# Attention weights scaled by ScalarE, head by head, at the head of the next slot, instead of by VectorE

## The reference

```python
s = jnp.einsum('btkgd,bjkd->bkgtj', qb, kc) * scale            # compressed keys
p_cmp = jax.nn.softmax(jnp.where(valid, s, NEG_INF), axis=-1) * valid
o_cmp = jnp.einsum('bkgtj,bjkd->btkgd', p_cmp, vc)
...
p = jax.nn.softmax(jnp.where(smask, s, NEG_INF), axis=-1)      # selected blocks
o_slc = jnp.einsum('bkgtn,bktnd->btkgd', p, vs)
...
p = jax.nn.softmax(jnp.where(wmask, s, NEG_INF), axis=-1)      # window
o_win = jnp.einsum('bkgtn,bnkd->btkgd', p, vw)
o = gb[..., 0:1] * o_cmp + gb[..., 1:2] * o_slc + gb[..., 2:3] * o_win
```

## Time and profile before

| | |
|---|---|
| median of 3 runs | 2523.26 us (2515.41 to 2525.65) |
| the profiled execution | 2526.35 us |
| its span, first to last instruction | 2524.6 us |
| busy in the span: PE, DVE, ACT, POOL | 2376.2 (94%), 1912.4 (76%), 1300.5 (52%), 277.4 us (11%) |
| mean granted clock of TensorE | 0.975 |
| slots 27 to 40 (layer 0) | about 303 to 443 us |
| slots 27 to 40 (layer 1) | about 1528 to 1661 us |

### The profile page before, as it was taken

One profiled execution on the slowest core, in us unless ns is written; L12 is line 12 of the kernel. 1 busy time (PEld: TensorE's weight loads), 2 busy tenths in 40 slices (PEclk: granted clock), 3 DMA queues, 4 the chain that ended last, 5 costly groups with the idle time before them and its releaser, 6 DMA issues.

```text
span 2524.6 us, 39922 instructions
## 1 busy us (share of the span) xinstructions
PE 2376.2 (94%) x13810; PEld 2060.3 (82%) x13810; DVE 1912.4 (76%) x2756; ACT 1300.5 (52%) x2117; POOL 277.4 (11%) x425
## 2 busy tenths in 40 slices
PE   4898889979999999999979999999899999999998
PEld 3788878757888888888869998886688888888886
DVE  7989987889999999766678976568897665565555
ACT  5265556446455455444466556654644444444444
POOL 1133211111111111000002130001010000000000
PEclk9998999999999999999989999999999999999999
DMA  9997858786998899777754764359596555556554
GB/s 389 398 334 276 301 200 266 257 318 236 345 352 321 324 340 331 272 266 269 273 212 143 262 237 161 115 201 355 205 354 219 186 187 183 186 188 187 194 193 151
DMA packets 197049, 643.04 MB, mean 255 GB/s; under 512 B 27249, under 2 KB 49905, under 8 KB 190913
## 3 DMA queue, kind: packets, MB, share of 16 engines
q1 hardware_dynamic: 125058, 421.72, 46.7%
q0 software_dynamic: 51264, 205.04, 22.9%
q10 hardware_dynamic: 20608, 14.72, 1.9%
HBM read 626.68 MB, written 14.71 MB: 254 GB/s over the span
## 4 chain that ended last, share of the span: by engine, by line
PE 75%; DVE 11%; DMA 6%; ACT 5%; issue 2%; SPq 1%; ACTq 0%; DVEq 0%; POOLq 0%
PE ps L1246 25%; PE ps L752 18%; PE ps L1247 13%; PE ps L735 10%; DMA ring<-stream 4%; DVE w_lo L1836 3%; PE ps L1126 3%; DVE ada_w L1842 2%; DVE mix L1836 2%; PE ps L800 2%; ACT w_hi L1307 1%; DMA ada_w<-ada_d 1%; SPq L535 1%; PE ps L1229 1%; PE ps L954 1%
## 5 line engine op out<-in xcount | busy, mean ns | idle before, releaser
L1836 DVE TENSOR_TENSOR w_lo<-ring,w_hi 128x1024 fp32r<-128x1024 f32 x720 | 893.8, 1245 | 485.9 <-ACT w_hi L1307 482.7
L1307 ACT ACTIVATE w_hi<-ring 128x1024 fp32r<-128x1024 f32 x720 | 761.4, 1059 | 837.4 <-PE ps L1247 351.1
L1246 PE MATMUL ps<-hT,w_hi 128*128 128x512 f32 x2688 | 947.3, 398 | 0.0
L1247 PE MATMUL ps<-hT,w_lo 128*128 128x256 f32 x2688 | 754.3, 281 | 0.0
L1246 PEld LDWEIGHTS ps<-hT,w_hi 128*128 128x128 f32 x2688 | 504.8, 188 | 124.7 <-DVE w_lo L1836 0.7
L1247 PEld LDWEIGHTS ps<-hT,w_lo 128*128 128x128 f32 x2688 | 507.9, 189 | 0.0
L735 PE MATMUL ps<-hT,w_hi 128*128 128x256 f32 x2176 | 414.7, 292 | 17.4 <-DVE w_lo L1836 15.8
L1842 DVE SCALAR_TENSOR_TENSOR ada_w<-ada_w,cs_row 128x1024 f32<-128x1024 f32 (+1 forms) x332 | 409.7, 1268 | 8.5 <-DMA ada_w<-ada_d 8.5
L735 PEld LDWEIGHTS ps<-hT,w_hi 128*128 128x128 f32 x2176 | 349.6, 197 | 28.1 <-issue 25.1
L735 PE MATMUL ps<-hT,w_lo 128*128 128x256 f32 x1088 | 312.9, 288 | 0.0
L605 POOL DMA_DIRECT2D ada_w<-ada_d x256 | 135.2, 528 | 1074.5 <-DVE ada_w L1842 1067.9
(11 more groups left out here) (306 smaller groups left out, 2420.2 us busy)
## 6 DMA issues: line engine op xcount, KB each, us to landing
ring<-stream SPq DMA_DIRECT2D x746, 512.0 KB, 4.5
ada_w<-ada_d POOLq DMA_DIRECT2D x320, 512.0 KB, 6.2
ada_w<-ada_d POOLq DMA_DIRECT2D x12, 1024.0 KB, 9.3
ada_lo<-ada_d POOLq DMA_DIRECT2D x10, 1024.0 KB, 11.9
ada_hi<-ada_d POOLq DMA_DIRECT2D x10, 1024.0 KB, 10.8
mix<-stream SPq DMA_DIRECT2D x14, 512.0 KB, 15.6
xs<-x SPq DMA_DIRECT2D x2, 2048.0 KB, 11.0
s_in_w<-mix ACTq DMA_DIRECT2D x8, 512.0 KB, 3.7
```

Source lines behind the costliest of these rows:

```text
L1246: pe.matmul(ps[:, bank, :], w_hi[:, s, ks], hT[:, k, :, :], start=k == 0, stop=False)
L1247: m = pe.matmul(ps[:, bank, SEQ:2 * SEQ], w_lo[:, s, ks], hT_hi[:, k, :], start=False, stop=k == KT - 1)
L1307: s.activation(w_hi[:, c % SPLIT, :], ring[:, at % RING, :], ACT.Copy).then_inc(hi_ready, 1)
L1836: return v.tensor_tensor(o, a, b, op)
```

## The change

For items of kind 1 and 2 the last product of `weighted` is taken from DVE. DVE now signals a new semaphore, `ns_w`, after the product of reciprocal and gate. ACT, in the next slot (28+m), behind its first `w_head` and ahead of `in_tile`, waits for `ns_w` and multiplies the exponentials head by head: four Copy instructions in place, with the column of `att_s` as the per-row scale. The last raises `ns_p`, for which the transposes wait as before. Items of kind 0 stay on DVE as they were. Since eight DVE instructions per layer no longer raise DVE's own step counter, its count falls from 210 to 202.

```diff
+        ns_w = Signal("ns_w", NI - NI // 3)
...
+                def weights_scaled(n):
+
+                    g, qt, kind = ITEMS[n]
+                    if kind == 0:
+                        return
+                    nk = (qt + 1) * P
+                    ns_w.wait(s, l, n - n // 3)
+                    for h in range(GQ):
+                        m = s.activation(pr[:, n % 2, h, 0:nk], pr[:, n % 2, h, 0:nk], ACT.Copy, scale=att_s[:, n % 2, 8 + h:9 + h])
+                    ns_p.by(m)
+
...
                     w_head(2 * n + AHEAD)
+                    if 0 <= n - ITEM_TILE - 1 < NI:
+                        weights_scaled(n - ITEM_TILE - 1)
                     in_tile(n)
                     w_head(2 * n + AHEAD + 1)
...
                     step(v.reciprocal(st3[:, 8:12], st3[:, 4:8]))
-                    step(tt(st3[:, 8:12], st3[:, 8:12],
-                            gates_t[:, qt, :].rearrange("p (h c) -> p h c", c=3)[:, GQ * g:GQ * (g + 1), kind], ALU.mult))
-                    w3 = st3[:, 8:12].unsqueeze(2).to_broadcast([P, GQ, nk])
+                    (ns_w.by if kind else step)(
+                        tt(st3[:, 8:12], st3[:, 8:12],
+                           gates_t[:, qt, :].rearrange("p (h c) -> p h c", c=3)[:, GQ * g:GQ * (g + 1), kind], ALU.mult))
                     if kind == 0:
+                        w3 = st3[:, 8:12].unsqueeze(2).to_broadcast([P, GQ, nk])
                         step(tt(p3, p3, w3, ALU.mult))
                         ok = K("cmp_valid", qt * NC, (qt + 1) * NC).unsqueeze(1).to_broadcast([P, GQ, nk])
                         ns_p.by(tt(p3, p3, ok, ALU.mult))
-                    else:
-                        ns_p.by(tt(p3, p3, w3, ALU.mult))
...
-DVE_STEPS, ACT_STEPS = 210, 8
+DVE_STEPS, ACT_STEPS = 202, 8
```

## The result

Over 12 runs each, interleaved on one chip, the changed kernel took 2533.11 us (median) and the kernel before 2517.18: a ratio of 1.0061, 95% interval 1.0039 to 1.0083, so 15.4 us slower (9.8 to 20.9). The profiled execution took 2541.89 us with a span of 2540.1, where that of before had 2524.6: 15.5 us more. Each of the two lies some 9 us over its kernel's median (8.8 and 9.2), so they can be read against each other for the typical difference. Behind the change the lines are one higher on PE and ACT (L1017 is L1018, L1019 is L1020, L1307 is L1308, L954 is L955) and DVE's helper L1836 is L1850.

A forecast was written before the change was run, and what follows sets the result against it. PE was taken to set the pace, except in a few slots of layer 0 where DVE is full. Lateness of 13.9 us plus 3.6 for clock spells gave 17.5 on 2523.3, so 2541 us, range 2528 to 2551.

The forecast's parts named there:

- The likeliest case: PE gets the products late in both attention stretches and idles trigger clock spells: 17.5 us slower, 2541 us, chance 0.60.
- DVE's and ACT's work: Sixteen products leave DVE, 15.3 us; 64 Copies come to ACT, about 24 us, four taking 1.29 or 1.72 us.
- the nearer bound: Scaled Copies priced like Exps of the same shapes with a per-row bias, 0.391 and 0.498 us, not like short Copies.
- Item 1: Its transposes on PE come 2.74 us late in layer 0, same pattern in layer 1; not carried on.
- Item 4: Its transposes on PE come 0.56 us late in layer 0 and 1.76 in layer 1, carried on from here.
- Items 5 and 10: Their four Copies are covered while ACT waits for PE, so costed at nothing.
- Items 7, 8 and 11: Late at PE by 2.44, 5.02 and 6.40 us in layer 0, by 3.31, 5.89 and 7.53 in layer 1.
- The clock: New PE idle before item 8 brings one slow-clock spell per layer, 1.8 us each, 3.6 us added.
- The waits: PE's transposes wait for ACT's product near 20 us over ten times, where 6.1 us stood against DVE.
- (b): DVE's relief wins at items 2 and 4: PE's idle and two clock spells go, 2514 us, chance 0.06.
- (a): The delay is swallowed in the slots; only item 4's lateness stays, 0.56 + 1.76 us: 2526 us, chance 0.20.
- (c): The clock falls after every new uncovered PE idle, six spells in place of two: +24.7 us, 2548 us, chance 0.14.

The follow-up runs named there:

- the two halves: The change with only items 7 and 8 on ACT: 2526.39 against 2520.48 us, ratio 1.0037; with all moved items but these: 2525.60 us, ratio 1.0029.
- the last kernel above: The changed kernel with ACT's wait for the gate row's DMA moved from the end of slot 34 to that of slot 35: 2528.92 against 2517.91 us.

## Why the prediction was right

The forecast was 2541 us from a base of 2523.3, +17.5; measured were 2533.11 us and +15.4 (9.8 to 20.9). The base of three runs stood 6 us over the 2517.18 of twelve; this, and not the change, is most of the 8 us between 2541 and 2533.11. The likeliest case came true, and by its steps:

- **DVE's and ACT's work**: -15.6 us for -15.3, +24.5 for about +24; four Copies in 1.26 and 1.69 us for 1.29 and 1.72. Taking the nearer bound was right; the Trainium skill's rule on the pointer operand (ScalarE: Activation LUTs, What ACT_TABLE_LOAD costs) gives an estimate of 386 and 492 ns, and the trace agrees: the 64 Copies of the two shapes took 384 to 506. The sum's 0.03 us for the semaphore was read from no row; from the product's end to PE's start the rows above give about 0.06 (357.92 + 1.69 against 359.67), and the Copies, 0.03 shorter than forecast, make up for it.
- **Item 1** 2.74 late, measured 2.72 and 2.93, and not carried on: 0.24 at item 3 of layer 0. In layer 1, 1.59 us were left at item 3, which the forecast didn't have; ACT's head of item 4 came 0.2 earlier against item 0 in both layers all the same, as assumed.
- **Item 4**: 0.52 and 1.72 us for 0.56 and 1.76.
- **Items 5 and 10**: no wait in either layer, at item 5 just so.
- **Items 7, 8 and 11** can't be read directly, as a clock spell went away behind item 4 (3.16 and 1.56 us) and the gate row landed 3.65 us later in layer 0. With both taken out of the shifts (a subtraction, not a run), item 7 has 2.43 and 3.46 for 2.44 and 3.31, item 8 has 5.84 and 5.98 for 5.02 and 5.89, and item 11 has 7.07 and 7.61 for 6.40 and 7.53. The 0.8 too much at item 8 of layer 0 is there in the projection tile that took 7.78 us at the low clock. The step that I called the weakest, that these items carry their lateness whole, held: 14.7 us so worked out, for 13.9.
- **The clock was the term that failed.** The forecast added a spell behind item 8 of either layer, +3.6, and kept those behind item 4. The trace has none behind item 4 and others behind items 1 and 7, partly under waits: about -4.7 us on the path instead of +3.6. A spell was priced at 1.8 us; the one that went away in layer 0 was worth 3.16. And 1.6 of the 4.7 also went away in layer 1 of kernels that leave item 4 as it was. The gate row's +3.65 and 1.8 us outside the stretches brought the profiled sum up again: 14.7 - 4.7 + 3.65 + 1.8 = 15.5. Half of the agreement of this one execution is such luck; the 12 runs' median of +15.4 and the two halves' +9.3 and +7.3 stand apart from it.
- **The waits** of PE: 19.8 us over nine times, for about 20 over ten. Item 8's idle was 0 and 0.84 us, not 2.4: item 7 had PE late enough already. It shows at 2.33 us in layer 0 of the kernel with items 7 and 8 alone, and at 2.27 in both layers where the gate row's wait was moved.

Of the rivals, (b) falls by the sign. (a) falls by the size: its +2.3 us lies below the interval (+9.8), and items 7, 8 and 11 carried their lateness. The Trainium skill's advice behind (b) (Perfetto Trace Analysis, Optimizing Scalar/DVE Operations: if DVE is saturated, offloading to Scalar may make sense) didn't carry here: leaving the work out altogether brought 5 us, moving it to ACT cost 15. (c) speaks of six spells in place of two but adds six, 10.8 us, and its +24.7 lies above the interval; four more would give 13.9 + 7.2 = 21.1, at its upper edge of 20.9, so that the time alone hardly excludes it. The trace speaks against it: spells did follow the idles behind items 1 and 7, but not item 4's 2.40 and 1.21 us, and the mean clock is as before.

Left open: what sets the time of the gate row's transfer, why a clock spell follows one idle and not the next, whether the change has a part in the spell that went away in layer 0 (it was away too in the last kernel above, with the same idle of 2.4 us there), and how much each of them moves the median.

## What to carry to other kernels

On an engine that goes through its list in strict order, moved work is priced by its place before its share of busy time: take the start of the instruction ahead of it, add the durations up to its end, and compare with the consumer's start in the old trace. If that end is later than the consumer's start, the difference is lost at that place, and is carried on wherever the engines run tied together. What the relief of the old engine can bring is quickly bounded by leaving the work out (here 5 us for 15.3), and should be known before the work is moved.

## What the runs showed of the hardware that I had not expected

The transfer of one small row of gates to HBM in slot 33 of layer 0 took from 11.8 to 16.8 us to land over the kernels of this study, and 16.8 and 13.7 us in two of them with the same code ahead of it. The granted clock fell to its lower level behind some idles of PE and not behind others of like length: full clock (1.00) behind 2.40 us at item 4 of after, 0.68 behind 2.11 us at the same place in before; and in layer 1, behind the same idle of 1.07 us at the same place, 0.69 in before and 1.00 in the kernel with items 7 and 8 alone. A forecast may put such spells in its range, but not one by one into its sum.
